# A conformer/attention/MoE layer: gate projections as seven block products, three quarters of the depthwise convolution in two token phases

## What is computed

```
proj = x @ w_in + b_in            # 4608 columns: glu 1024 | q 512 | k 512 | v 512 | gate logits 2048
u = a * sigmoid(gate)             # GLU, 512 channels
u = depthwise causal conv(u, width 31) + b_dw
y_conv = silu(layer_norm(u)) @ w_conv_out
y_attn = chunked_attention(q, k, v, rel_bias) @ w_attn_out
g_conv, g_attn = split(sigmoid(gate_logits))
x = layer_norm(ALPHA * x + (g_conv * y_conv + g_attn * y_attn) @ w_o + b_o)
x = layer_norm(ALPHA * x + grouped_moe(x))      # 16 experts, top 2 in the best group
```

## Time and profile before

| | us |
|---|---|
| median of 3 runs | 1134.77 |
| lowest, highest | 1133.7, 1134.91 |
| profiled execution, span from first to last instruction | 1130.7 |
| median less that span | 4.1 |
| granted TensorE clock, mean, as a share of full speed | 0.991 |
| DMA, mean over the span | 177 GB/s |

### The profile page before, as it was taken

One profiled execution on the slowest core, in us unless ns is written; L12 is line 12 of the kernel. 1 busy time (PEld: TensorE's weight loads), 2 busy tenths in 40 slices (PEclk: granted clock), 3 DMA queues, 4 the chain that ended last, 5 costly groups with the idle time before them and its releaser, 6 DMA issues.

```text
span 1130.7 us, 17012 instructions
## 1 busy us (share of the span) xinstructions
PE 1098.3 (97%) x5583; PEld 913.1 (81%) x5584; DVE 803.2 (71%) x1152; ACT 529.2 (47%) x787; POOL 227.4 (20%) x190
## 2 busy tenths in 40 slices
PE   8999999999999999999999999999999999999984
PEld 7888888888978789878888888787888888888762
DVE  5799999935447766666685588888679556558866
ACT  5111111123456665645331134467578545557755
POOL 0000000000046864757100000013121211212110
PEclk9999999999999999999999999999999999999998
DMA  7121233232111010181632325889999876699966
GB/s 266 56 84 56 83 104 104 83 112 93 57 38 43 19 43 1 65 326 39 251 118 88 142 119 196 278 331 354 324 331 381 311 230 192 236 352 341 368 177 269
DMA packets 49800, 199.58 MB, mean 177 GB/s; under 512 B 7249, under 2 KB 7633, under 8 KB 47682
## 3 DMA queue, kind: packets, MB, share of 16 engines
q1 hardware_dynamic: 43538, 176.19, 41.9%
q0 software_dynamic: 6192, 22.49, 8.0%
HBM read 166.21 MB, written 32.52 MB: 176 GB/s over the span
## 4 chain that ended last, share of the span: by engine, by line
PE 85%; DVE 4%; DMA 4%; ACT 3%; POOL 2%; issue 2%; ACTq 0%; DVEq 0%; SPq 0%; POOLq 0%
PE ps L544 16%; PE ps L546 16%; PE ps L545 16%; PE ps L1570 9%; PE ps L1572 9%; PE ps L1571 9%; PE ps L644 2%; PE ps L630 2%; DMA gu<-in_wexp 2%; PE ps L616 2%; DMA dn_raw<-in_wexp 2%; PE ps L1651 1%; PE ps L1566 1%; POOL pr L499 1%; PE ps L1678 1%
## 5 line engine op out<-in xcount | busy, mean ns | idle before, releaser
L544 PE MATMUL ps<-xh,wh 128*128 128x512 f32 x512 | 203.3, 397 | 2.0 <-DVE xl L1030 1.7
L545 PE MATMUL ps<-xl,wh 128*128 128x512 f32 x512 | 199.5, 390 | 0.0
L546 PE MATMUL ps<-xh,wl 128*128 128x512 f32 x512 | 199.5, 390 | 0.0
L1469 DVE TENSOR_TENSOR gu<-gu (+1 forms) x128 | 148.6, 1220 | 33.6 <-issue 21.5
L499 POOL TENSOR_SCALAR pr<-pr,rinv 128x640 f32<-128x640 f32 (+4 forms) x64 | 95.4, 1503 | 379.7 <-DVE rinv L1153 379.5
L1052 DVE SCALAR_TENSOR_TENSOR cv<-u,dw_t,cv 128x1024 f32<-128x1024 f32 x120 | 154.1, 1284 | 3.7
L1570 PE MATMUL ps<-gu,xgh 128*128 x336 | 134.0, 399 | 4.0 <-DVE gu L1469 2.2
L1463 ACT ACTIVATE gu<-gu (+1 forms) x128 | 124.4, 1048 | 20.6 <-DMA gu<-in_wexp 13.0
L1572 PE MATMUL ps<-gu,xgl 128*128 x336 | 131.9, 393 | 0.0
L1571 PE MATMUL ps<-gu,xgh 128*128 x336 | 131.4, 391 | 0.0
L544 PEld LDWEIGHTS ps<-xh,wh 128*128 128x128 f32 x512 | 96.1, 188 | 25.4 <-issue 6.4
(11 more groups left out here) (278 smaller groups left out, 2022.4 us busy)
## 6 DMA issues: line engine op xcount, KB each, us to landing
gu<-in_wexp SPq DMA_DIRECT2D x64, 1024.0 KB, 9.1
dn_raw<-in_wexp SPq DMA_DIRECT2D x16, 2048.0 KB, 9.8
raw<-in_wblk SPq DMA_DIRECT2D x52, 512.0 KB, 4.2
gate_cols<-gst SPq DMA_DIRECT2D x16, 512.0 KB, 5.3
xf<-acc_rows SPq DMA_DIRECT2D x8, 512.5 KB, 8.1
xraw<-in_xT SPq DMA_DIRECT2D x8, 512.0 KB, 7.3
gcm<-gate_cols SPq DMA_DIRECT2D x8, 512.0 KB, 7.5
gam<-gate_cols SPq DMA_DIRECT2D x8, 512.0 KB, 14.5
```

Of the source, the lines that this page charges most:

```text
L544: pe.matmul(o, a_h, b_h, start=first, stop=False)
L545: pe.matmul(o, a_h, b_l, start=False, stop=False)
L546: return pe.matmul(o, a_l, b_h, start=False, stop=last)
L1469: eng.tensor_tensor(gu[:, par, k, 1, :], gu[:, par, k, 1, :].bitcast(F32), gu[:, par, k, 0, :], ALU.subtract).then_inc(gu_lo, 1)
```

## The change

Gates. The two gate columns of one index q (conv gate and attention gate) form a 2 x 2 block problem: two output blocks, two halves of the inputs, two halves of the tokens. Instead of eight block products, seven are made from sums and differences of weight quarters and of token quarters (`ORDER`, `PARTS`, `SUMS`); a product has 4 input chunks x 3 = 12 matmuls of 512 columns, 56 in all. The weight sums are made ahead from memory to memory by GpSimd: 64 DMAs of 256 KB, 32 plain copies and 32 that add while they write, in seven rounds, each waiting for the one before. The input sums are four VectorE operations over 4 x 512 elements, with high and low parts of their own. Quarters of weights ("units") come through eight slots, four products ahead of their use. Seven additions on VectorE per pair combine the products in `gst`; the sigmoid follows there, and gates are stored by quarters.

Convolution. Channel block 0 keeps 31 taps over 1024 tokens, but writes its sum with even tokens in the first half of the row and odd tokens in the second. Blocks 1 to 3 are done in two phases (even and odd taps, and their sum): 16 + 15 + 16 taps over 512 or 513 tokens, one sum ahead and three combinations, 51 operations a block. Taps are spread over the steps by `conv_work`: seven whole or fourteen half operations per block step, two half operations per product, three per value tile.

Order. Mean and variance move behind the values and into the Q/K stage. The reciprocal is cut in four, three of them in attention slots 0 to 2; the normalisation goes to slots 3 to 6, the four silus to slot 7 on ScalarE. GpSimd scales the first two bias tiles. Several semaphores are merged.

The core of the diff, shortened:

```diff
-TAPS_A_STEP = 7
+HP = (CW + 1) // 2
+WHOLE, HALVED = CW, 2 * HP + HP - 1 + 4
+WORK_A_STEP, WORK_A_PRODUCT, WORK_A_VALUE = 14, 2, 3
+SILU_SLOT = 7
...
+UNIT_SLOTS = 8
+PARTS = {1: (0, 0), 2: (0, 1), 4: (1, 1)}
+SUMS = {5: 0, 6: 1, 7: 2, 3: 3}
+ORDER = (1, 6, 5, 7, 2, 3, 4)
...
+                def weight_sums(g, stage):
+
+                    if not 0 <= g < KC // 2:
+                        return
+                    for q in (2 * g, 2 * g + 1):
+                        s1, s2, s3, s4 = (wsum_dram[i, q] for i in range(4))
+                        of = (((s1, gate_weights(q, 1, 0)), (s3, gate_weights(q, 0, 0)), (s2, gate_weights(q, 0, 0)), (s4, gate_weights(q, 0, 1))),
+                              ((s1, gate_weights(q, 1, 1)), (s3, gate_weights(q, 1, 0))), ((s2, s1),), ((s4, s2),))[stage]
+                        for o, a in of:
+                            if stage:
+                                pool.dma_start(o, a, accum_op=ALU.add, max_dma_last_dim=4096).then_inc(wsum_in, 16)
+                            else:
+                                pool.dma_start(o, a).then_inc(wsum_in, 16)
+
+                for r in range(KC // 2 + 3):
+                    if r:
+                        pool.wait_ge(wsum_in, 16 * sums_issued(r - 1))
+                    for stage in range(4):
+                        weight_sums(r - stage, stage)
+                scale_bias(0)
+                scale_bias(1)
...
+                def gate_product(m):
+
+                    x, q = UNITS[m]
+                    s, bank = m % UNIT_SLOTS, m % 8
+                    pe.wait_ge(u_lo, m + 1)
+                    if m < 8:
+                        pe.wait_ge(u_ready, CB - 1 + (m >= 4))
+                    else:
+                        bank_read(m - 8)
...
-                for g in range(LAST_GATES[0]):
-                    gate_job(g)
-                conv_mean()
-                gate_job(LAST_GATES[0])
-                conv_var()
-                gate_job(LAST_GATES[1])
+                for m in range(N_UNITS):
+                    gate_product(m)
...
+                pe.wait_ge(v_lo, TT)
+                conv_mean()
...
+                        if i and h == 0:
+                            conv_var()
...
+                def conv_late(n):
+
+                    if n == SILU_SLOT:
+                        for j in range(CB):
+                            act.wait_ge(nrm, j + 5)
+                            act.activation(cv[:, j, :], cv[:, j, :], ACT.Silu, scale=cpar[:, 1, j:j + 1],
+                                           bias=cpar[:, 2, j:j + 1]).then_inc(silu_done, 1)
...
+                def conv_tap(k):
+
                     if k == 0:
+                        dve.wait_ge(u_ready, 1)
+                    tap, w, o = phases(u[:, 0, k:k + SEQ]), dw_t[:, 0, k:k + 1], by_phase(cv[:, 0, :])
...
+                    i -= 1
+                    if i < 3 * HP - 1:
+                        which, k = (0, i) if i < HP else (1, i - HP) if i < 2 * HP - 1 else (2, i - 2 * HP + 1)
+                        if which == 0:
+                            o, tap, w = first, u[:, j, 2 * k:2 * (k + HALF) + 1:2], dw_t[:, j, 2 * k:2 * k + 1]
+                        elif which == 1:
+                            o, tap, w = even, u[:, j, 2 * k + 1:2 * (k + HALF) + 1:2], dw_t[:, j, 2 * k + 1:2 * k + 2]
+                        else:
+                            o, tap, w = odd, u[:, j - 1, k:k + HALF], dw_2[:, j, k:k + 1]
...
+                for m in range(N_UNITS):
+                    if m + 4 < N_UNITS:
+                        unit_low(m + 4)
+                    elif m + 4 < N_UNITS + 2:
+                        low(B_V[0] + m + 4 - N_UNITS)
+                    if m == 0:
+                        glu(CB - 1)
+                    if m:
+                        gate_sums(m - 1)
+                    conv_work(WORK_A_PRODUCT)
+                gate_sums(N_UNITS - 1)
```

More of the change, by code:

```diff
@@ L59, in block_columns @@
         cols += [a + j, g + j]
-    cols += [gate + j for j in range(N_GATE)]
     cols += [v, v + 1, q, k, q + 1, k + 1, q + 2, k + 2, v + 2, v + 3, q + 3, k + 3]
-    return cols
+    return cols, [gate + j for j in range(N_GATE)]
 C_ID, C_TRI, C_IOTA, C_TOK, C_THR, C_SPARE, C_EARLIER, C_SLOT, C_UPTO = 0, 128, 256, 388, 396, 404, 405, 421, 456
@@ L289, in place, with gate_weights, sum_round, sums_issued @@
                 i = n - B_WO
-                return wh2[:, i], wl2[:, i], raw2[:, i], raw2_in[i], 16
+                return wh2[:, i], wl2[:, i], raw2[:, i], raw2_in[i], 48 if i < 2 else 16
             s = n % RING
             return wh[:, s], wl[:, s], raw[:, s], raw_in[s], 16 * ((n if n < B_WO else n - 4) // RING + 1)
+        def gate_weights(q, n, k):
+            return wblk[W_GATE + 2 * q + n][:, CB * k:CB * k + CB, :]
+        def sum_round(x, q):
+            return q // 2 + {5: 1, 7: 1, 6: 2, 3: 3}[x]
+        def sums_issued(r):
+            return sum(2 * many for g in range(KC // 2) for stage, many in enumerate((4, 2, 1, 1)) if g + stage <= r)
+        U2, W, U3, C22, C11, C12, C21 = range(1, 8)
+        def sum_no(which, q):
+            return 7 * q + which
+        def sigmoids_at(m):
+            if not 0 <= m - 2 < N_UNITS:
+                return []
+            x, q = UNITS[m - 2]
+            return [(q, slot) for after, slot in ((7, 3), (2, 0), (3, 2), (4, 1)) if after == x]
+        SIGMOIDS = [x for m in range(N_UNITS + 2) for x in sigmoids_at(m)]
+        def sigmoid_no(q, slot):
+            return SIGMOIDS.index((q, slot)) + 1
+        V_BANKS = (0, 1, 2, 3)
         def tiles_of(c):
@@ L899, in v_high @@
+                for m in range(N_UNITS + 2):
+                    if m < N_UNITS:
+                        copy_product(m)
+                    if m + 4 < N_UNITS:
+                        unit_high(m + 4)
+                    elif m + 4 < N_UNITS + 2:
+                        high(B_V[0] + m + 4 - N_UNITS)
+                    for q, slot in sigmoids_at(m):
+                        gate_sigmoid(q, slot)
                 def v_high(s, t, o):
@@ L952, in _ @@
                 for i in range(2):
-                    act.wait_ge(gs_out[i], 16 * KC)
+                    for slot in range(4):
+                        act.wait_ge(row_moved[4 * i + slot], GATES_STORED)
                 def conv_high(n):
@@ L2176, in two_a_block @@
         return columns(w).reshape(KC // 2, 2, P, CB, P).transpose(0, 2, 1, 3, 4).reshape(KC // 2, P, KC, P)
-    blocks = np.concatenate([columns(w_in)[block_columns()], two_a_block(w_conv_out), two_a_block(w_attn_out), columns(w_o)])
+    first, gates = block_columns()
+    w_in = columns(w_in)
+    blocks = np.concatenate([w_in[first], two_a_block(w_conv_out), two_a_block(w_attn_out), columns(w_o), w_in[gates]])
     rel = np.clip(np.arange(P)[:, None] - np.arange(BANDW)[None, :] + 512, -256, 256) + 256
```

495 lines of the change are left out of this document (322 added, 173 removed).

## The result

| | before | after |
|---|---|---|
| median of the runs compared, us | 1134.24 (4 runs) | 1176.65 (4 runs) |
| lowest, highest | 1132.82, 1134.91 | 1174.64, 1178.41 |
| span of the profiled execution | 1130.7 | 1172.8 |
| granted TensorE clock, mean | 0.991 | 0.972 |

The ratio is 1.0374, 95% interval [1.0356, 1.0391]: 42 us slower. The prediction, 1133 us in a range up to 1158, was wrong in sign and in size.

What follows compares the result with a forecast made beforehand. VectorE was taken to share the bound with TensorE, busy 289 of about 318 us before attention, so its queue was followed. 1134.8 - 6.3 (earlier scores) + 4.4 (silus) = 1132.9 us; range 1117 to 1158.

Steps and rivals of the forecast that it cites:

- unpriced item: 31 whole taps alternating between two row halves: lower bound 1.284 us a tap, which was taken; upper +33 us in all.
- Rival A: The alternation in the 31 whole taps costs time, all on VectorE's queue: +16 us gives 1149, the full doubling 1166; chance 0.25.
- Start: Eight memory-to-memory copies beside the x loads: first block +3 us, bounds 0 and +10; block 5's low part at 46.2.
- Block steps: Six VectorE steps after block 5's low part: 66.9 us, ending at 113.1; product 4 starts at 113.7.
- Product stage: VectorE's 18.7 us per pair level with TensorE's 19.05; values start at 259.1, 13.8 us earlier than before.
- Values to mean: VectorE ends the value stage at 286.2, TensorE's value tiles at 282.1; GpSimd's bias scaling is needed 50 us later.
- Mean to scores: Mean, Q/K and variance after 286.3: 1.7 + 21.9 + 1.7 us, so scores start at 311.6, 6.3 earlier than before.
- Attention: Silus in slot 7: 7.2 us less 1.95 idle and 0.9 slack, about +4.4; reciprocals and normalisations hidden, price 0.
- the fixed costs have eaten it: Convolution on VectorE: 164 us before, 162 us with three blocks halved, despite a quarter fewer multiplications.
- Sums through memory: GpSimd's fourth round of weight sums ready at 99, needed by about 112: 13 us of cover, no wait.
- The wait before the mean: TensorE waits 4.2 us for the last value low part before the mean, a new wait.

Runs made afterwards that it cites:

- e3_late: The changed kernel with GpSimd's weight-sum DMAs held back until the x columns are split; 1170.79 us, ratio 1.0297 to the kernel before.
- e4_three: The changed kernel with whole taps written in order, bias scaling after the second Q half, and weight sums held until x is split; 1133.68 us, ratio 1.001.
- e7_bias: The changed kernel with whole taps written in order and GpSimd's first two bias scalings moved after the second Q half; 1142.54 us, ratio 1.0086.
- e14_lock: The kernel before with eight GpSimd scalings of an unused buffer beside VectorE's first taps; one run, 1140.55 us.
- e15_spread: e4_three with the mean after the first Q half and 124 whole taps in token order, a second tap in eleven product steps; 1132.01 us, ratio 0.998.

## Why the prediction was wrong

**The step that failed** is the unpriced item: "Lower bound: as the rows, 1.284 ... I take the lower value". The alternating write costs 0.82 us for 1024 elements, and the whole tap takes 2.16. The 26 to 27 us of 30 taps arrive in full, since VectorE's queue is the path. My reason, that 64- and 128-wide runs with gaps show no cost, was about steps between long runs, and the tap moves at every element. Rival A had the mechanism, was given 0.25, and was capped at 2 x 0.528 more for a tap; 0.88 lies in that. Even its dearest case, 1166, is 10 us short of 1176.65: the start, the bias scaling and attention, below, came on top. The Trainium skill, Vector Engine (DVE) Microarchitecture Reference, section Measured stream behaviour on trn2, had been cited for it: by its 1.71 ns for the write the taps cost 21 us more, an estimate; the runs gave 27. By its rule on the write, the trace agrees. On reads it was cited too broadly: the full rate is that of an operation with one source, and for two sources, one of them hopping 4 KiB at every element, the section gives 1.73 ns. By that, the trace does not agree: a tap with one read alternating by 2 KB took 1.33 us, 1.285 in order. Between a rule with a number and a weak reason without one, I chose the reason.

**Stage by stage**, the prediction's ledger and what was measured:

- *Start.* "I take +3 us for the first block, bounds 0 ... and +10". The middle columns of x came 2.4 us apart instead of 1.28, and block 5's low part 7.1 later than worked out. Against e3_late, where no copy runs beside the x loads, it is 53.30 - 45.17 = 8.1: the copies cost 8, near the upper bound, and the rest of that ledger was 2 short.
- *Block steps.* 66.9 us were worked out from 46.2 to 113.1. The GLU due at 113.7 came at 146.65: 7.1 from the start, and 26 more from the thirty taps. With the three edits of e4_three it came at 111.0.
- *Product stage.* From that GLU to the first value 259.1 - 113.7 = 145.4 predicted, 291.53 - 146.65 = 144.9 measured. The costing of unit low parts, combined results and half operations was right.
- *Values to mean.* 27.2 predicted, 30.9 measured. "GpSimd's bias scaling ... needed at the first score, 50 us later" looked at when its result is due and not at what it does to VectorE. Two scalings hold VectorE's operations for 2.6 us each; without them (e7_bias) scores came 6.1 us earlier.
- *Mean to scores.* 25.3 predicted, 27.1 measured. The fp32 matmuls of the mean took 0.80 to 1.06 us instead of 0.59, after TensorE's wait and at a lower granted clock (0.60 from 322 to 326, shown below).
- *Attention.* "+4.4, bounds 0 and 7.2"; 9.0 measured. The silus are 6.4 of it: of their 7.2 us only 0.8 was covered, where I had counted 1.95 of idle time and 0.9 of slack. 2.7 us stay without them. I had priced reciprocals and normalisations at 0, hidden; the normalisation took 1.86 us in the mean instead of 1.22. Two of the four are long, 2.76 us at 364.28 and 2.24 at 383.23; both began while GpSimd subtracted a weight's low part (363.56 to 365.97, 381.98 to 384.39) and ended about one plain normalisation after it, which is the pattern of e14_lock. That this makes the 2.7 us is argued, not shown.

Summed: the values 32.4 later than predicted, 3.7 and 1.8 up to the scores, 4.6 in attention: 42.5 of the 43.7 us between 1132.9 and 1176.65.

**What held, and what was luck.** TensorE does 96 matmuls less, 21.8 us at the pace of before. With the three unwanted costs taken out, half of that shows at the scores (307.0 against 317.85), and attention takes nearly all of it back (171.3 us against 161.0): VectorE and the silus bound what TensorE could gain. Of the halved convolution, "the fixed costs have eaten it": e15_spread confirms it. Sums through memory were in time, 92.5 for my 99. The wait before the mean, 3.9 us for 4.2, is partly luck: the bias scaling made up for part of it, and in e4_three it is 1.6. So is the median of e4_three, 1133.7 for my 1132.9: its scores came 4.6 us earlier than predicted and its attention took 6 us longer.

## What to carry to other kernels

Where an edit changes the order in which elements are written, measure or look up that order before anything else is added up: here one `rearrange` decided some 27 of 42 us, and swapping its two dimensions cost nothing. When VectorE is the bound, GpSimd's operations on SBUF and any DMAs put beside the first loads have a price on VectorE's queue, however early their results are; put them where VectorE is idle or reads one operand from PSUM, if the kernel has such a place. And before a saving on one engine is worth its cost in work for another, sum up the second engine's queue: 21.8 us of TensorE for some 50 of VectorE ended, at its best, 2.5 us ahead.

## What the runs showed of the hardware

- A 1024-wide scalar_tensor_tensor takes 1.285 us with all operands in order or in steps of two, 1.33 with a read that alternates between two rows 2 KB apart, 2.11 with such a write, 2.18 with both, 2.07 with the sum in steps of four.
- A GpSimd tensor_scalar of 3.87 us in SBUF lets one VectorE operation through; a tensor_scalar that takes 0.81 us alone took 4.08, and a tap 3.93 for 1.28. Operations with one operand in PSUM were not held: in attention of the changed kernel, with GpSimd busy for 104 of 170 us, none of the 36 low parts of 512-wide transposed probabilities took over 0.694 us, and two of them took 1.29 at 374.19, inside two scalings of GpSimd from 372.83 to 376.58.
- Eight 256 KB memory-to-memory copies at the start raised four distances between the arrivals of 512 KB loads from 1.28 us to between 2.4 and 2.8. The copies' issue took 4.39 us for eight, 0.55 each, half of the 1.065 of the gather by which I had priced them.
- TensorE's granted clock fell behind its waits. Around the values it waited 2.1 us before 311.0 and 3.9 before 322.4. From 312.7 to 315.9 the matmuls of the values took 0.41 us instead of 0.28, and three of the mean's four took 1.06 instead of the 0.59 of the earlier trace rows; from 323 to 326 the granted clock was 0.50, the lower of its two levels, 1.2 of 2.4 GHz. All of the earlier trace rows has 1.00. In e7_bias, with a wait of 2.7 us there, the clock stayed at 1.00 and the median of the mean's matmuls at 0.59. Two windows of the changed kernel:

```profile
314.00:318.00 4.00, 4.00 (x28) 4.00 (x27) 3.90 (x7) 0.38 (x1) 0.00 (x0) 0.75 0.00 0
322.00:326.00 4.00, 3.62 (x6) 1.68 (x7) 0.55 (x2) 0.00 (x0) 0.00 (x0) 0.60 0.19 78
```
